# Two stacked transformer blocks on one core: opening loads, rotary tables and first modulation made into one block

## The reference, cut to what matters

```python
def _rope(x, positions):
    half = x.shape[-1] // 2
    inv = ROPE_THETA ** (-jnp.arange(half, dtype=jnp.float32) / half)
    ang = positions.astype(jnp.float32)[..., None] * inv
    ...
    cos = jnp.cos(ang).astype(x.dtype)
    sin = jnp.sin(ang).astype(x.dtype)

def first_block(x, c, positions, ada_w, ada_b, norm_mix_w, w_in, ...):
    c_act = jax.nn.silu(c)
    for l in range(DEPTH):
        mod = (c_act @ ada_w[l] + ada_b[l])[:, None, :]
        sh1, sc1, g1, sh2, sc2, g2 = jnp.split(mod, 6, axis=-1)
        h = _rmsnorm(x, norm_mix_w[l]) * (1 + sc1) + sh1
        x = x + g1 * _mixer(h, positions, w_in[l], ...)
        ...
```

## Time and profile before

| | |
|---|---|
| median of three runs | 2271.33 us (2256.76 to 2271.38) |
| the profiled execution's own time | 2259.08 us |
| its span, first to last instruction | 2257.2 us |
| PE busy | 1987.9 us (88%) |
| DVE busy | 1441.3 us (64%) |
| ACT busy | 1100.1 us (49%) |
| hardware DMA queue | 445.41 MB, 55.2% of 16 engines' span |
| mean granted clock of PE | 0.937 |

### The profile page before, as it was taken

The page is one execution under the profiler, slowest core; times in us unless marked ns, Lnnn a source line. Parts: engine busy times, 40 slices in busy tenths (PEclk is TensorE's granted clock), DMA queues, the critical chain, the costliest instruction groups (busy, mean ns, idle before and its releaser), DMA issues. The chain is left out here.

```text
span 2257.2 us, 37023 instructions
## 1 busy us (share of the span) xinstructions
PE 1987.9 (88%) x15254; PEld 1670.8 (74%) x15254; DVE 1441.3 (64%) x1794; ACT 1100.1 (49%) x1334; POOL 146.7 (7%) x151
## 2 busy tenths in 40 slices
PE   4698899899788899899959895898899999999997
PEld 3586677899577677799848664786778788787785
DVE  0264445786355444688547939765788788788886
ACT  0253343655253343466346433222567677676773
POOL 0000000000000000000004613720000000000000
PEclk9799999999899879899979997899899999999998
DMA  8775364545266237444342120000689899799895
GB/s 320 284 240 164 103 224 141 218 178 185 104 219 217 94 126 248 166 157 183 131 136 91 56 73 11 14 20 11 229 297 378 298 350 378 270 369 337 311 380 219
DMA packets 153800, 447.54 MB, mean 198 GB/s; under 512 B 10032, under 2 KB 12720, under 8 KB 151088
## 3 DMA queue, kind: packets, MB, share of 16 engines
q1 hardware_dynamic: 153648, 445.41, 55.2%
HBM read 444.33 MB, written 1.05 MB: 197 GB/s over the span
## 5 line engine op out<-in xcount | busy, mean ns | idle before, releaser
L212 DVE TENSOR_TENSOR me_wlow<-me_w,me_whigh 128x2048 fp32r<-128x2048 f32 (+1 forms) x203 | 451.8, 2247 | 108.0 <-ACT me_whigh L207 107.8
L207 ACT ACTIVATE me_whigh<-me_w 128x2048 fp32r<-128x2048 f32 (+1 forms) x203 | 380.1, 1884 | 134.3 <-PE ps L220 126.3
L218 PE MATMUL ps<-me_whigh,me_xhigh 128*128 128x512 f32 x512 | 207.1, 404 | 12.0 <-PEq L119 12.0
L218 PE MATMUL ps<-up_xhigh,ffn_whigh 128*128 128x256 f32 x704 | 201.8, 287 | 8.1 <-DVE ffn_wlow L212 6.5
L220 PE MATMUL ps<-me_whigh,me_xlow 128*128 128x512 f32 x528 | 208.4, 395 | 0.0
L219 PE MATMUL ps<-me_wlow,me_xhigh 128*128 128x512 f32 x512 | 201.9, 394 | 0.0
L219 PE MATMUL ps<-up_xlow,ffn_whigh 128*128 128x256 f32 x704 | 201.0, 286 | 0.0
L220 PE MATMUL ps<-up_xhigh,ffn_wlow 128*128 128x256 f32 x704 | 200.9, 285 | 0.0
L212 DVE TENSOR_TENSOR ffn_wlow<-ffn_w,ffn_whigh 128x2048 fp32r<-128x2048 f32 (+1 forms) x72 | 149.3, 2110 | 60.8 <-ACT ffn_whigh L207 60.6
L212 DVE TENSOR_TENSOR mix_wlow<-mix_w,mix_whigh 128x1024 fp32r<-128x1024 f32 (+2 forms) x116 | 140.3, 1213 | 69.5 <-ACT mix_whigh L207 69.2
L207 ACT ACTIVATE ffn_whigh<-ffn_w 128x2048 fp32r<-128x2048 f32 (+1 forms) x72 | 123.2, 1759 | 47.8 <-PE ps L220 47.8
(11 more groups left out here) (665 smaller groups left out, 4212.5 us busy)
## 6 DMA issues: line engine op xcount, KB each, us to landing
me_w<-w_exp_gate SPq DMA_DIRECT2D x34, 2048.0 KB, 9.8
me_w<-w_exp_up SPq DMA_DIRECT2D x34, 2048.0 KB, 10.2
me_w<-w_exp_down SPq DMA_DIRECT2D x32, 2048.0 KB, 10.1
mix_w<-w_mix SPq DMA_DIRECT2D x108, 512.0 KB, 4.2
mix_aside<-ada_w SPq DMA_DIRECT2D x96, 512.0 KB, 4.3
ffn_w<-ffn_w_up SPq DMA_DIRECT2D x20, 2048.0 KB, 7.7
ada_w<-ada_first SPq DMA_DIRECT2D x12, 2048.0 KB, 22.6
ffn_w<-ffn_w_down SPq DMA_DIRECT2D x8, 2048.0 KB, 7.9
```

Source lines behind the costliest of these rows:

```text
L207: return nc.scalar.activation(high, x, ACT.Copy)
L212: return nc.vector.tensor_tensor(low, x, high.bitcast(F32), ALU.subtract)
L218: nc.tensor.matmul(out, lh, rh, start=start, stop=False)
```

## The change

The opening blocks and `modulation` are replaced by one block, `opening`. In it SP issues the vectors and `base` first, then pieces 0 to 4 of the weights, then the positions and `consts`, then pieces 5 to 11, each with its wait for a slot as before, and x last; it waits for x at the end. GpSimd clears the wide tile and sets `ones` at once. ACT waits for the first two loads, makes the silu, and takes sine and cosine after its copy of share 9. DVE computes the angles after its copy of share 6. The operations themselves are the same. The scratch tiles of the rotary tables now live beside the weights' slots.

```diff
-def modulation(core, what, w, vectors, wide, mod, quad_pick):
+def opening(core, w, vectors, wide, mod, quad_pick, ones, pos, inv, cos, sin, first, middle, last):
...
             @block.gpsimd
             def _(pool):
                 nc.gpsimd.memset(wide, 0.0).then_inc(cleared, 1)
+                nc.gpsimd.memset(ones, 1.0).then_inc(ones_set, 1)
+                pool.wait_ge(ones_set, 1)
 
             @block.sync
             def _(sp):
+                for to, source in first:
+                    sp.dma_start(to, source).then_inc(first_here, 16)
                 for j in range(n):
                     if j >= slots:
                         sp.wait_ge(shares, j - slots + 1)
                     sp.dma_start(raw[:, j % slots], w[4 * j:4 * j + 4].rearrange("q p f -> p q f"))\
                         .then_inc(landed[j % slots], 16)
+                    if j == middle_at:
+                        for to, source in middle:
+                            sp.dma_start(to, source).then_inc(middle_here, 16)
+                for to, source in last:
+                    sp.dma_start(to, source).then_inc(last_here, 16)
+                sp.wait_ge(last_here, 16 * len(last))
...
             @block.scalar
             def _(act):
                 act.wait_ge(cleared, 1)
+                act.wait_ge(first_here, 16 * len(first))
                 nc.scalar.activation(wide[:, :, 0:2], ..., ACT.Silu).then_inc(silu, 1)
                 for j in range(1, n, 2):
                     act.wait_ge(shares, j + 1)
                     nc.scalar.activation(rows[:, j, :], core.ps[:, j % banks, :], ACT.Copy).then_inc(rows_s, 1)
+                    if j == 9:
+                        act.wait_ge(reduced, 1)
+                        nc.scalar.activation(sin, sin, ACT.Sin).then_inc(rotary_done, 1)
+                        nc.scalar.activation(cos, cos, ACT.Sin).then_inc(rotary_done, 1)
 
             @block.vector
             def _(dve):
+                def angles():
+                    dve.wait_ge(middle_here, 16 * len(middle))
+                    order(V.tensor_copy(posf[:, :], pos))
...
                 for j in range(0, n, 2):
                     dve.wait_ge(shares, j + 1)
-                    nc.vector.tensor_copy(rows[:, j, :], core.ps[:, j % banks, :]).then_inc(rows_v, 1)
+                    V.tensor_copy(rows[:, j, :], core.ps[:, j % banks, :]).then_inc(rows_v, 1)
+                    if j == 6:
+                        angles()
...
-        load(core, "first_vectors", [(vectors[:, :], I["first_vectors"])])
-        modulation(core, "ada", I["ada_first"], vectors, wide[:, :, :], mod_next, k["quad_pick"])
+        opened["first"].insert(0, (vectors[:, :], I["first_vectors"]))
+        opening(core, I["ada_first"], vectors, wide[:, :, :], mod_next, k["quad_pick"], **opened)
...
-            load(core, "inputs", [(x[:, :, :], I["x"].rearrange("b (t p) d -> p (b t) d", p=P)),
-                                  (base[:, :], cv[:, 0:P + 2]), (consts[:, :], cv[:, P + 2:n_consts]),
-                                  (pos[:, :], I["positions"])])
...
+            opened = dict(ones=ones[:, :], pos=pos[:, :], inv=k["inv_freq"], cos=cos, sin=sin, first=[(base[:, :], cv[:, 0:P + 2])],
+                          middle=[(pos[:, :], I["positions"]), (consts[:, :], cv[:, P + 2:n_consts])],
+                          last=[(x[:, :, :], I["x"].rearrange("b (t p) d -> p (b t) d", p=P))])
+            first_block(core, I, k, mod_next, x, opened)
```

More of the change, by code:

```diff
@@ L440 @@
 QW = P // QUADS
-def modulation(core, what, w, vectors, wide, mod, quad_pick):
+def opening(core, w, vectors, wide, mod, quad_pick, ones, pos, inv, cos, sin, first, middle, last):
     nc = core.nc
     n = ADA_PIECES // 4
[L449 to L455, removed]
+    slots, banks, middle_at = 5, 4, 4
+    width = ROPE // 2
+    two_pi = 2 * np.pi
+    c1 = 6.28125
+    c2 = float(np.float32(np.round((two_pi - c1) * 2 ** 21) / 2 ** 21))
+    c3 = float(two_pi - c1 - c2)
+    pi = 3.1415925
+    magic = 12582912.0
+    with ExitStack() as mem, core.section() as sem:
+        raw = core.sb(mem, "ada_w", [P, slots, 4, DM])
+        rows = core.sb(mem, "ada_rows", [P, n, 512])
+        posf = core.sb(mem, "posf", [P, TT])
+        ang, turns, over = (core.sb(mem, i, [P, TT, width])[:, :, :] for i in ("ang", "turns", "over"))
+        first_here, middle_here, last_here = sem("first_here"), sem("middle_here"), sem("last_here")
+        landed = [sem(f"ada_landed{s}") for s in range(slots)]
+        cleared, ones_set, silu, shares, rows_v, rows_s, summed, added = (sem(f"ada_{i}") for i in (
+            "cleared", "ones", "silu", "shares", "rows_v", "rows_s", "summed", "added"))
+        own, reduced, rotary_done = (sem(f"rotary_{i}") for i in ("order", "reduced", "done"))
+        with nc.Block(no_gpsimd_drain=True) as block:
             @block.gpsimd
@@ L506, in _ @@
                     nc.scalar.activation(rows[:, j, :], core.ps[:, j % banks, :], ACT.Copy).then_inc(rows_s, 1)
+                    if j == 9:
+                        act.wait_ge(reduced, 1)
+                        nc.scalar.activation(sin, sin, ACT.Sin).then_inc(rotary_done, 1)
+                        nc.scalar.activation(cos, cos, ACT.Sin).then_inc(rotary_done, 1)
             @block.vector
             def _(dve):
+                V, order = nc.vector, Order(dve, own)
+                def angles():
+                    dve.wait_ge(middle_here, 16 * len(middle))
+                    order(V.tensor_copy(posf[:, :], pos))
+                    order(V.tensor_tensor(ang, posf[:, :].unsqueeze(2).to_broadcast([P, TT, width]),
+                                          inv.unsqueeze(1).to_broadcast([P, TT, width]), ALU.mult))
+                    order(V.tensor_scalar(turns, ang, 1.0 / two_pi, None, ALU.mult))
+                    order(V.tensor_scalar(turns, turns, magic, None, ALU.add))
+                    order(V.tensor_scalar(turns, turns, magic, None, ALU.subtract))
+                    for c in (c1, c2, c3):
+                        order(V.scalar_tensor_tensor(out=ang, in0=turns, scalar=-c, in1=ang, op0=ALU.mult, op1=ALU.add))
+                    order(V.tensor_scalar(sin, ang, pi, -pi, ALU.min, ALU.max))
+                    order(V.tensor_scalar(ang, ang, np.pi / 2, None, ALU.add))
+                    order(V.tensor_scalar(over, ang, np.pi, two_pi, ALU.is_gt, ALU.mult))
+                    order(V.tensor_tensor(ang, ang, over, ALU.subtract))
+                    V.tensor_scalar(cos, ang, pi, -pi, ALU.min, ALU.max).then_inc(reduced, 1)
@@ L510, in _ @@
                 for j in range(0, n, 2):
                     dve.wait_ge(shares, j + 1)
-                    nc.vector.tensor_copy(rows[:, j, :], core.ps[:, j % banks, :]).then_inc(rows_v, 1)
+                    V.tensor_copy(rows[:, j, :], core.ps[:, j % banks, :]).then_inc(rows_v, 1)
+                    if j == 6:
+                        angles()
                 dve.wait_ge(summed, n)
-                nc.vector.tensor_tensor(mod, core.ps[:, 4, 0:96].rearrange("p (m v) -> p m v", v=2),
-                                        vectors[:, 0:48].unsqueeze(2).to_broadcast([P, 48, 2]), ALU.add)\
-                    .then_inc(added, 1)
+                V.tensor_tensor(mod, core.ps[:, 4, 0:96].rearrange("p (m v) -> p m v", v=2),
+                                vectors[:, 0:48].unsqueeze(2).to_broadcast([P, 48, 2]), ALU.add).then_inc(added, 1)
@@ L630, in turn_features @@
     products(core, what, tiles, turn, out, odd)
[L633 to L671, removed]
 def rotate(nc, order, x1, x2, cos, sin, tmp):
@@ L2143, in _, with first_block @@
                 in_turn(gate_dve(dve), norm_dve(dve), first_dve(dve), main_dve(dve))
-def first_block(core, I, k, mod_next, x):
+def first_block(core, I, k, mod_next, x, opened):
     nc = core.nc
```

8 lines of the change are left out of this document (removed).

## The result

The changed kernel takes 2252.53 us in the median of 20 runs (2241.39 to 2263.83), the kernel before 2267.95 us in 20 (2256.76 to 2276.24). The ratio is 0.9944, with a 95% interval of 0.9929 to 0.9959: 12.7 us faster (9.3 to 16.1), 0.6%, inside the range and inside 1%. The ratio is estimated over all runs and isn't the quotient of the two medians, which lie 15.4 us apart.

A forecast was written before the change was run, and what follows sets the result against it. The opening was taken as bound by bytes: 25.17 MB of weights at 408 GB/s, 61.7 us, started late. Weights 13.67 us earlier less 2.43 for constants give -11.24 us, 2271.33 to 2260.1 us; range 2243 to 2267.

The forecast's parts named there:

- Weights 13.67 us earlier: Opening, SP's queue: first piece of weights issued third, at 1.73 us instead of 15.40, so weights start 13.67 us earlier.
- Constants 2.43 us on the path: Between pieces 4 and 5: 0.992 MB of constants and positions at 408 GB/s delay pieces 5 to 11 by 2.43 us.
- Vectors and base for nothing: Start of SP's queue: 97 KB, 0.24 us of DMA, pass while the third DMA is being issued; cost 0.
- Rival A: Opening: small loads hold up the first piece by 3.4 us, leaving -7.8 us, 2263.5 us; chance 0.07.
- x for nothing: Behind piece 11: x's 2.6 us of DMA hide behind share 11, the add-ups and DVE; cost 0.
- The angles, sine and cosine for nothing: Rotary tables: DVE's 2.8 us between copies of shares 6 and 8, ACT's between shares 9 and 11; cost 0.
- The sum, -11.24 us: At `mod_next`: -13.67 + 2.43 = -11.24 us, so 74.96 us instead of 86.20.
- Rival B, the slow tail: Share 11 and add-ups fall on the slow clock, 2.5 us more: -8.7 us, 2262.6 us; chance 0.14.
- Rivals C and D, one drop of the clock less or more: Layer loop: C saves 9.0 to 12.8 us more, 2251.1 to 2247.3, chance 0.21; D gives +1.6, 2272.9 us, chance 0.12.
- Two passes that differ from 516 and 529 us: Layer loop: sign of being wrong, if its two passes took other times than in the first profile.
- The predicted median, 2260.1 us: Whole kernel: median of the runs shown, 2271.33 us, less 11.24 us; chance of this forecast 0.43.
- The forecast against the profiled execution's own time, 2247.8 us: Whole kernel: the profiled execution's 2259.08 us by its own clock would become 2247.8 us.

The follow-up runs named there:

- the old order in one block: Changed kernel with x, base, constants, positions and vectors all ahead of the first piece of weights, still one block; 2256.13 us, ratio 0.9964 against the kernel before.
- the constants last: Changed kernel with positions and constants behind piece 11, just ahead of x, angles after share 10; 2251.10 us, run again 2248.05 us, ratios 0.9939 and 0.9922 to before.
- The version filled by 16: Changed kernel with 16 additional small PE matmuls behind each of shares 0 to 9, into a PSUM bank nobody reads; 2257.90 us, ratio 0.9965 to before.
- hole after piece 5: Changed kernel with positions and constants one piece later, between pieces 5 and 6; 2258.43 us in one run.
- the doubled constants: Changed kernel with the 968 KB of constants loaded a second time between pieces 4 and 5, into a tile nobody reads; 2262.47 us in one run.

## Why the prediction was right, and where it was not

*Weights 13.67 us earlier.* Share 0 came 13.80 us earlier; the first piece was issued at 1.65 and not 1.73, because vectors and base were issued in 0.40 and 0.42 us where x and base had taken 0.44 and 0.46. Right.

*Constants 2.43 us on the path.* Shares 5 to 11 came 11.25 us earlier by the profiles, 13.80 - 11.25 = 2.55 us for constants and positions; doubled, they cost 2.40 more; taken off the path they gave back 2.30 and 2.62. Right.

*Vectors and base for nothing.* Base landed at 3.2 us and not at 6.0, since x no longer stood ahead of it, the silu was done at 4.7 and not at 7.5, share 0 wasn't held. Rival A is out: it would have put share 0 at 13.5. *x for nothing.* It landed at 72.4, and SP then waited 4.1 us for PE. Right. *The angles, sine and cosine for nothing.* They lie between copies, and the wait of PE ahead of shares 7 to 11 is that of the weights. Right. ACT even saved its second table load: silu and sine stand in one block behind a single load of 1.28 us.

*The sum, -11.24 us.* At share 11 it is -11.25 between the first profiles and -10.9 between the second ones. But the sum was stated for `mod_next`, and there it is -9.78 and -10.74: in the first pair the slow tail of the changed kernel met the fast one of before. In the times it is -12.7 us (-9.3 to -16.1) and, with the kernel run once more, a ratio of 0.9956, -10.0 us (-5.7 to -14.5). Both intervals hold -11.24.

*Rival B, the slow tail, had a chance of 0.14.* That was too little, and the step behind it was wrong. I read the fast share 11 of one profile as a property of the kernel before, and the slow one as something that the change might bring. Of twelve profiles four have the fast tail (5.93 to 6.46 us), six the slow one (7.31 to 7.56) and two a slower one yet (9.36, 10.07), and the kernel before has one of each of the first two. Two profiles each can't tell whether the change makes a slow tail more frequent. I priced it at 2.5 us, with the add-ups at 1.35 us for eight; the measured prices are 1.5 us where only share 11 is slow, and up to 4.1 where the 24 of the add-ups are too, at 5.28 us: the 1.35 for eight weren't all at the slow clock.

*Rivals C and D, one drop of the clock less or more.* Two passes that differ from 516 and 529 us were named as a sign of being wrong, and they came at 530 and 526. The sign was a bad one: the kernel before, run again, took 531.5 us from copy to copy where it had taken 520.8. I priced them from two passes of one execution, 12.8 us apart, and took 2257 and 2271 us for two levels. The size is right and the picture of two levels is not. Over the 66 runs of the kernel before that ran beside the experiments, the times run from 2245.67 to 2276.42 us, between 2257 and 2271 us with no gap above 1.4 us, and they go with the mean granted clock of their run: the correlation is -0.90, and 0.001 of clock goes with 1.5 us. By itself 0.001 more of mean clock is 4.5 us less at 1.2 GHz in 2260 us, and half of that is 2.3 us; so, as an estimate, about two thirds of the slow time stands on the path. In one least-squares fit over the 164 runs whose clock is on record, with a common slope of -1.42 us for each 0.001, the changed kernel stands 11.4 us (+-1.3) under before in its first 20 runs and 12.6 (+-1.6) in the next 12, the old order in one block 8.0 (+-1.6), the constants last 11.6 (+-2.1) and 14.8 (+-1.8). The kernel before, run again, comes out 2.0 (+-1.6) above itself, so the fit is no better than some 2 us. The version filled by 16 comes out at only -0.7 (+-1.7), where its own ratio says -7.9: its filling raises the mean clock (0.935 in its 12 runs, 0.930 before) without saving time, and the fit doesn't hold for it. It is a fit, not an experiment: that the clock makes the spread, and doesn't only go with it, is shown for the opening alone, where filling set the clock to 1.00 and the shares to 1.95 us.

*The predicted median, 2260.1 us*, was 7.6 us too high. Of this 3.4 us are in the base: the three runs shown had a median of 2271.33, the twenty have 2267.95. The other 4.2 us are the difference of the two medians, 15.4, less the predicted 11.24, and lie within the scatter of the twenty runs. The forecast against the profiled execution's own time, 2247.8 us, missed by 14 us, because the one profile had the shortest first pass of twelve and the other the longest (520.8 and 534.9). Both misses are one error: three runs and one profile were taken as the kernel's time, and they scatter by more than the effect. That the times show 12.7 us where no landmark of this pair of kernels shows more than 11.25 lies within the interval too, and the mechanism doesn't say it.

What stays open: what decides, from run to run of one program, which stretch meets 1.2 GHz. The place of the constants alone doesn't (hole after piece 5, one profile). Nor does the old opening seem to favour the loop: run again, it had a first pass of 531.5 us, and the mean granted clock is 0.930 both over the 66 runs of before and over 32 of the changed kernel.

## What to carry to other kernels

When a stage is bound by one long stream of bytes, the only question for everything around it is whether it stands ahead of the last byte in the queue: each megabyte ahead of it cost 2.4 us, x behind it cost nothing and the constants at most 0.5 us, and the emptied queue at the start (no data from 8.6 to 15.4 us but the 32 KB of vectors, then a second start-up) cost 8.8 us. Put them into one block, so that no barrier empties the queue, in the order in which they are needed. And read a gain of this size at a landmark right behind the edit, where it repeated within 0.35 us, not at the end of one profile, where a first pass that varied by 14 us hid it.

## What the runs showed of the hardware

- SP is held when it issues far ahead of the data. Five pieces (10.5 MB) took 9.51 us to issue, and the 1 KB of positions behind them 5.35 us, where the same 1 KB took 0.43 us to issue in the kernel before. The queue stayed full, so nothing was lost here. What it would cost on an engine with other work wasn't tried.
- Matmuls of 32 columns that go round the four column groups pass every 30 ns (64 in 1.95 us at the full clock); the fillings, all in one group, took 114 ns each (32 in 3.66 us). That is a factor of 3.75 between matmuls of the same shape. The groups are the likely reason, but the fillings also all write one place in PSUM, and no run takes the two apart.
- A single core drew 407 to 409 GB/s from HBM from 20 to 60 us in every version. The Trainium skill, "DMA: Bandwidth & Descriptors", section "Where 436 GB/s comes from", gives about 358 for the HBM side, as one core's half of what a stack delivers; no run here, with one core alone, shows such a limit, and the doubled constants cost what 408 says.
- A PE that is busy for 27 of 40 us between pieces of weights goes back and forth between 1.2 and 2.4 GHz, mostly with a slow and a fast share in turn (mean 0.82); busy for 40 of 40 it stays at 2.4. The Trainium skill, "TensorE: Matmul & The Clock Gate", section "HAM oscillation — how this bites in real kernels", tells of a matmul kernel that waits for its loads and falls back to the slow clock in each wait. The trace agrees that the clock falls and rises between loads, but not with the pattern: here mostly every second share was fast.
